# The u-table products of a hybrid SSD, attention and PEER block: wide and narrow matmuls interleaved, where they ran in two passes

## The reference

```python
q = (xf @ wq).reshape(t, PEER_HEADS, 2, PEER_HALF)
sc = jnp.einsum("thpk,hpnk->thpn", q, keys)
s1, i1 = lax.top_k(sc[:, :, 0], PEER_TOPK)
s2, i2 = lax.top_k(sc[:, :, 1], PEER_TOPK)
...                                  # top 16 of the 16 x 16 sums: experts eidx, softmax: gate
act = jax.nn.gelu(jnp.einsum("thkd,td->thk", u_tab[eidx], xf), approximate=False)
out = jnp.einsum("thk,thkd->td", gate * act, v_tab[eidx])
```

## Time and profile before

| | |
|---|---|
| Time, median of 3 runs | 1729.22 us (1729.13 to 1729.28) |
| Profiled execution | 1729.22 us, of which the span from first to last instruction is 1727.4 |
| TensorE busy | 1711.7 us, 99% of the span |
| VectorE, ScalarE, GpSimd busy | 1326.5, 919.5, 531.8 us |
| Mean rate of the DMAs | 258 GB/s |

### The profile page before, as it was taken

The page is one execution under the profiler, slowest core; times in us unless marked ns, Lnnn a source line. Parts: engine busy times, 40 slices in busy tenths (PEclk is TensorE's granted clock), DMA queues, the critical chain, the costliest instruction groups (busy, mean ns, idle before and its releaser), DMA issues.

```text
span 1727.4 us, 27916 instructions
## 1 busy us (share of the span) xinstructions
PE 1711.7 (99%) x10171; PEld 1514.4 (88%) x10171; DVE 1326.5 (77%) x2178; ACT 919.5 (53%) x1567; POOL 531.8 (31%) x336
## 2 busy tenths in 40 slices
PE   9999999999999999999999999999999999999997
PEld 8999999999888888888888888888888888888885
DVE  7878878767999999555555666668878888888887
ACT  6545755444554554544444444455555555555556
POOL 0000000000007887877783000058545412111210
PEclk9999999999999999999999999999999999999999
DMA  7654568776657888777787888899999999999984
GB/s 259 217 199 160 172 189 278 226 237 206 201 195 192 191 194 204 200 190 199 197 191 207 263 264 266 265 361 337 360 343 358 363 362 353 367 360 365 361 331 142
DMA packets 186550, 445.79 MB, mean 258 GB/s; under 512 B 59361, under 2 KB 94449, under 8 KB 177905
## 3 DMA queue, kind: packets, MB, share of 16 engines
q1 hardware_dynamic: 146976, 373.47, 64.2%
q0 software_dynamic: 39504, 71.55, 15.6%
HBM read 423.79 MB, written 20.57 MB: 257 GB/s over the span
## 4 chain that ended last, share of the span: by engine, by line
PE 97%; DMA 1%; DVE 1%; ACT 0%; SPq 0%; issue 0%; DVEq 0%
PE ps L1736 27%; PE ps L1740 14%; PE ps L2115 7%; PE ps L2113 7%; PE ps L2111 7%; PE ps L2099 7%; PE ps L2101 7%; PE ps L1767 4%; PE ps L1769 4%; PE ps L1768 4%; PE ps L1950 3%; PE ps L1951 3%; PE ps L1952 3%; DMA big<-x_t 1%; PE ps L2064 0%; DMA raw<-w_in 0%
## 5 line engine op out<-in xcount | busy, mean ns | idle before, releaser
L960 DVE TENSOR_TENSOR low<-raw,high 128x1024 fp32r<-128x1024 f32 x378 | 460.2, 1222 | 85.6 <-ACT high L644 76.6
L1736 PE MATMUL ps<-acts,high 128*128 128x512 f32 x2048 | 488.7, 391 | 0.0
L644 ACT ACTIVATE high<-raw 128x1024 fp32r<-128x1024 f32 x378 | 395.2, 1051 | 86.7 <-PE ps L1769 38.4
L1736 PEld LDWEIGHTS ps<-acts,high 128*128 128x128 f32 x2048 | 376.4, 188 | 73.0
L637 ACT ACTIVATE high<-raw 128x1024 fp32r<-128x1024 f32 x172 | 182.3, 1061 | 171.1 <-PE ps L2115 171.1
L1740 PEld LDWEIGHTS ps<-acts,low 128*128 128x128 f32 x2048 | 262.6, 191 | 10.0
L1740 PE MATMUL ps<-acts,low 128*128 128x256 f32 x2048 | 265.7, 283 | 0.0
L598 POOL DMA_INDIRECT big<-v_tab,half_sb x64 | 108.3, 1692 | 492.9 <-DVE big L1641 298.3
L967 DVE TENSOR_TENSOR low<-raw,high 128x1024 fp32r<-128x1024 f32 x172 | 206.3, 1222 | 64.4 <-ACT high L637 64.2
L578 POOL DMA_INDIRECT gate_scratch<-gates_sb,cells_sb x128 | 209.6, 1637 | 67.6 <-issue 67.6
L865 ACT ACTIVATE side<-ps 128x256 f32<-128x256 f32 x128 | 49.1, 383 | 274.5 <-PE ps L1740 274.2
(11 more groups left out here) (286 smaller groups left out, 3203.1 us busy)
## 6 DMA issues: line engine op xcount, KB each, us to landing
raw<-u_tab SPq DMA_DIRECT2D x256, 512.0 KB, 4.2
raw<-v_tab SPq DMA_DIRECT2D x172, 512.0 KB, 7.2
raw_more<-v_tab SPq DMA_DIRECT2D x84, 512.0 KB, 7.1
raw<-w_in SPq DMA_DIRECT2D x62, 512.0 KB, 3.5
raw<-w_out SPq DMA_DIRECT2D x32, 512.0 KB, 4.9
raw<-w_q SPq DMA_DIRECT2D x32, 512.0 KB, 4.9
gate_scratch<-side SPq DMA_DIRECT2D x32, 384.0 KB, 5.8
big<-gate_scratch SPq DMA_DIRECT2D x16, 768.0 KB, 7.2
```

Source lines behind the costliest of these rows:

```text
L644: nc.scalar.activation(slot(high, s), slot(raw, s), ACT.Copy).then_inc(hi_done, 1)
L960: V.tensor_tensor(slot(low, s), slot(raw, s), slot(high, s).bitcast(F32), ALU.subtract).then_inc(lo_done, 1)
L1736: mm(both, tile_of(high, kk), both_tiles(kk), start=(kk == 0), stop=False, skip_group_check=True)
```

## The change

`paired_product` goes. The paired chunks take the ordinary loop over halves and slices of `product`: for each half one wait for `lo_done`, then for each of its 8 slices one wide matmul and at once the narrow one of the same slice. There is no wait for `hi_done` any more (the low half is made from the high one, so `lo_done` implies it). `used` is raised behind the last narrow matmul of either half. The count and the shapes of the matmuls stay as they are. PSUM's bank is again opened by the first wide matmul.

```diff
-            def paired_product(c, par, acc, ready):
-
-                both = ps[:, par, :]
-                tile_of = lambda t, kk: t[:, 2 * par * PIECE + kk * P:2 * par * PIECE + (kk + 1) * P]
-                for kk in range(KT):
-                    if kk % 8 == 0:
-                        pe.wait_ge(hi_done, 2 * c + kk // 8 + 1)
-                    if ready is not None and kk in READY_AT:
-                        pe.wait_ge(tile_lo, ready + READY_AT[kk])
-                    mm(both, tile_of(high, kk), both_tiles(kk), start=(kk == 0), stop=False, skip_group_check=True)
-                for kk in range(KT):
-                    if kk % 8 == 0:
-                        pe.wait_ge(lo_done, 2 * c + kk // 8 + 1)
-                    ins = mm(acc, tile_of(low, kk), hi_tile(kk), start=False, stop=(kk == KT - 1), skip_group_check=True)
-                    if kk % 8 == 7:
-                        ins.then_inc(used, 1)
-
             def product(c, par, midway=None, ins_hi=None, ins_lo=None, ready=None, late=None,
                         paired=False):
...
-                if paired:
-                    paired_product(c, par, acc, ready)
-                    return
                 for half in range(2):
                     s = 2 * par + half
                     pe.wait_ge(lo_done, 2 * c + half + 1)
...
                         wh = high[:, s * PIECE + k * P:s * PIECE + (k + 1) * P]
                         wl = low[:, s * PIECE + k * P:s * PIECE + (k + 1) * P]
-                        mm(acc, wh, a_hi, start=(kk == 0), stop=False)
-                        mm(acc, wh, a_lo, start=False, stop=False)
-                        ins = mm(acc, wl, a_hi, start=False, stop=(kk == KT - 1))
+                        if paired:
+                            mm(ps[:, par, :], wh, both_tiles(kk), start=(kk == 0), stop=(kk == KT - 1),
+                               skip_group_check=True)
+                        else:
+                            mm(acc, wh, a_hi, start=(kk == 0), stop=False)
+                            mm(acc, wh, a_lo, start=False, stop=False)
+                        ins = mm(acc, wl, a_hi, start=False, stop=(kk == KT - 1), skip_group_check=paired)
                     ins.then_inc(used, 1)
```

## The result

The changed kernel took 1740.14 us (median of 4 runs, 1740.10 to 1740.20), the kernel before beside it 1729.25 us (1729.13 to 1729.33). By the medians it became slower by 10.9 us, a ratio of 1.0063. Over all executions on record the ratio is 1.0059, with a 95% interval of 1.0044 to 1.0075; they include two more of the changed kernel, at 1739.69 and 1736.79 us. No trace of the faster one was kept, so what follows explains the profiled execution (1740.11 us) and those that agree with it. The forecast was 1728.1 us. 1740 lies within the wide range that was given (1724 to 1746), but outside the forecast's own (1726 to 1732), on the side of rival A.

The account below looks back on a forecast made before the run. TensorE's matmul stream was taken to bound the kernel. Chunks 45 to 127 saving 1.66 us and a wait adding 0.55 gave -1.1 us, so 1728.1 us; own range 1726 to 1732, wide range 1724 to 1746.

Parts of the forecast that it names:

- rival A: Paired chunks: step behind every narrow matmul is slow, narrow gives nothing back; 0.007 us per pair, 1741 us; chance 0.32.
- I take t = 0: Paired chunks: a wide-narrow pair costs nothing above 0.2266 + 0.1200 us, so each chunk takes 0.02 us less.
- The wait: TensorE needs VectorE's low halves earlier; waiting near chunk 43 during routing delays chunk 45, +0.55 us.
- The zeros: Instruction count, clock, weight loads, earlier-freed slots and work queued on other engines: no added time.
- the large figure: Wide weight load behind a narrow matmul sticks out by 68 ns, 139 us in all; the prediction rejected it.
- B: Paired chunks: every wide-narrow pair pays the whole 0.02 us; +38 us, 1768 us; chance 0.07.
- C: Paired chunks: pairs cost less than unmixed steps, 0.18 us saved per chunk after chunk 44; 1715 us; chance 0.13.
- D: Routing near chunk 43: VectorE falls further behind, 1 us more adds 1 to 2; 1729 to 1731; within forecast's 0.48.

Follow-up runs that it names:

- flip_late: The kernel before, but from chunk 52 on every odd chunk runs its narrow pass first: 1728.77 us against 1729.47, ratio 0.9996.
- narrow_128: The changed kernel with narrow matmuls of 128 columns instead of 256: 1719.13 us.
- three_narrow: The changed kernel with each wide matmul split into two of 256 columns, so 48 of one width per chunk: 1754.04 us beside 1728.98 of the kernel before.

## Why the prediction was wrong

*The sum's main term, "I take t = 0", failed.* A pair costs 0.0067 us over the unmixed steps, so 16 x 0.0067 - 0.02 = +0.087 per chunk and +11.1 us, where the prediction had -0.02 per chunk. The argument for 0 was that the slow steps have another wide matmul ahead, while both border steps looked ordinary. In the trace of after every wide step is slow (0.232 or more), though a narrow matmul follows it. In the traces of before, after and flip_late a wide step is slow only where a narrow matmul stands shortly ahead of it, whatever comes behind; in flip_late the wide group behind a wide one has no slow steps. The border step from wide to narrow in the kernel before comes after 16 wide steps, when the group has long settled, so it was no evidence on a stream that has a narrow matmul ahead of every wide one.

*Rival A was right in place and in net size.* It had +0.092 per chunk and 1741 us, with a chance of 0.32 against 0.48. Its reason, that a mix never leaves the first steps of a group, is only in part what the rows show. The step that follows a wide start averages 0.2365 over 60 late chunks of the trace, 0.0098 over, and the one that follows a narrow start 0.1168, 0.0032 under, though A had the narrow ones give nothing back. That the two come to A's 0.007 is partly luck. Nor does the stream stay unsettled. Unrounded, the wide steps are 0.241, 0.236 and 0.233 in turn (within 0.001), a cycle of three pairs (1.06 us) that repeats from 700 to 1100 us; the first of them is longer than any step of a group before (0.236 at most). And by A's picture groups of two would have been as slow, which they aren't.

*The wait was priced right, and had next to no part in the result.* Alone it gives chunk 43 a start at 656.80 for 656.84 forecast, and +0.48 us at chunk 45 for +0.55. In the changed kernel the slower matmuls hide it, as rival A's text said. What is left of it is 0.1 us at chunk 1, where the prediction had 0.05 at chunk 2. The sum also let the short stall of before (0.2 us near 656) stand, and the changed kernel lost it.

*The zeros held.* VectorE's and ScalarE's busy times moved by 1.4 and 0.2 us, GpSimd's by 12.8 off the chain; no row shows an effect of the slots that come free earlier; the expert-row stage kept its length: from its first matmul to the span's end 1738.3 - 1141.9 = 596.4 us, before 1727.4 - 1131.0 = 596.4. The weight load of 188 ns behind a step of 120 doesn't add its 68 ns, by far: the excess is a tenth of that. The estimate of 107 ns after the Trainium skill (TensorE: Matmul & The Clock Gate, LDWEIGHTS) was right to reject the large figure, and narrow_128 agrees: behind its short matmuls it is 0.108 us from one load's start to the next. Whether a load has any part in the 0.0067 us no run separates.

*Rivals B, C and D.* B's 0.02 per pair holds for groups of 8 and 16 and is three times too much for single ones. C has no support: no pattern with widths 512 and 256 ran under 5.547 per chunk. D didn't occur.

*What stays open* is the mechanism: why 512 with 256 costs 0.0067 in turn, 0.003 in groups of two, 0.020 in long groups, why 512 with 384 costs 0.013 and 384 with 256 nothing (by the estimate), and why one execution of the changed kernel took 3.4 us less than the rest.

## What to carry to other kernels

Where TensorE is the whole chain, the order of matmuls of different widths is a cost of its own: a few nanoseconds per change, 4096 matmuls, 11 us. Take the pitch of such a mixed stream from a run of the very pattern, since neither the unmixed pitches nor the steps at a group's border foretold it (long passes: 5.567 us a chunk, twos 5.573, fours 5.613, singles 5.653). And when one engine is slowed, look at what its former stalls were: here the slower stream swallowed a wait of half a microsecond that the same edit would have brought.

## What was not expected of the hardware

- Alternating matmuls of 512 and 256 columns take 0.3533 us a pair, 0.0067 more than their own streams' steps, in one PSUM bank or two; when neighbours read different columns the price stays (5.64 us per chunk). Turning between high and low weights costs nothing by itself (0.1200 per matmul in three_narrow). Pairs of 384 and 256 take 0.293, no more than the estimated sum.
- Groups of two (0.6967 us for 2 + 2) lose half of what singles lose per pair of changes, and a fifth of what groups of four do (1.403 us for 4 + 4).
- A group of wide matmuls behind another wide one needs no run-in: 3.79 us for 16 in flip_late against 3.82 behind narrow ones.
